# Sums of squares ahead of a norm: eight rows added on VectorE and one summed over the partitions on TensorE, in place of three

## The reference

```python
def _rmsnorm(x, g):
    x32 = x.astype(jnp.float32)
    y = x32 * lax.rsqrt(jnp.mean(jnp.square(x32), axis=-1, keepdims=True) + EPS)
    return (y * g.astype(jnp.float32)).astype(x.dtype)

def _modulate(x, g, shift, scale):
    return _rmsnorm(x, g) * (1.0 + scale) + shift

for l in range(DEPTH):
    ...
    x = x + gt1 * o                                                        # o: the mixed output times w_out
    x = x + gt2 * _swiglu(_modulate(x, g_ffn[l], sh2, sc2), w_ffn_in[l], w_ffn_out[l])
    ...                                                                    # xc likewise, in layer 0 alone
return _rmsnorm(x, g_final)
```

## Time and profile before

| what | us |
|---|---|
| median of 3 runs | 2006.08 (2005.21 to 2007.08) |
| profiled execution, its own time | 2007.02 |
| its span in the trace | 2005.2 |
| TensorE matmul busy | 1977.7 (99%) |
| TensorE weight load busy | 1671.6 (83%) |
| VectorE busy | 1354.1 (68%) |
| ScalarE busy | 898.5 (45%) |
| GpSimd busy | 821.0 (41%) |

### The profile page before, as it was taken

One profiled execution on the slowest core, in us unless ns is written; L12 is line 12 of the kernel. 1 busy time (PEld: TensorE's weight loads), 2 busy tenths in 40 slices (PEclk: granted clock), 3 DMA queues, 4 the chain that ended last, 5 costly groups with the idle time before them and its releaser, 6 DMA issues.

```text
span 2005.2 us, 29242 instructions
## 1 busy us (share of the span) xinstructions
PE 1977.7 (99%) x11034; PEld 1671.6 (83%) x11034; DVE 1354.1 (68%) x2356; ACT 898.5 (45%) x1400; POOL 821.0 (41%) x355
## 2 busy tenths in 40 slices
PE   8999999999999999999999999999999999999998
PEld 5778788888888778777878887777899999999997
DVE  5894644567878867787885544689747878644555
ACT  4787544322122252235222212589855344555444
POOL 1002322344434444444344443500546886454443
PEclk9999999999999999999999999999999999999999
DMA  8222211222222334543544452322323555454554
GB/s 339 81 84 84 84 44 62 84 92 97 88 101 84 105 126 184 192 154 141 207 172 180 179 210 102 148 82 78 135 106 128 188 188 187 171 188 156 185 187 146
DMA packets 38699, 278.32 MB, mean 139 GB/s; under 512 B 4416, under 2 KB 4416, under 8 KB 5312
## 3 DMA queue, kind: packets, MB, share of 16 engines
q1 hardware_dynamic: 38592, 276.87, 37.6%
HBM read 275.80 MB, written 1.05 MB: 138 GB/s over the span
## 4 chain that ended last, share of the span: by engine, by line
PE 91%; DVE 3%; ACT 2%; POOL 1%; issue 1%; DMA 1%; SPq 0%; DVEq 0%; POOLq 0%; ACTq 0%
PE PS L513 90%; POOL WL L468 1%; PE PS L786 1%; DMA RAW<-in_stream 1%; ACT WH L878 1%; DVE PS L1325 0%; DMA CD<-in_lruw 0%; DVE CD L1325 0%; ACT PS L878 0%; DVE PS L1328 0%; DVE LT L1328 0%; PE PS L611 0%; ACT TMP L878 0%; ACT HH L878 0%; DVE HL L1328 0%
## 5 line engine op out<-in xcount | busy, mean ns | idle before, releaser
L468 POOL TENSOR_TENSOR WL<-RAW,WH 128x1024 fp32r<-128x1024 f32 x336 | 809.8, 2429 | 1159.6 <-ACT WH L878 1159.4
L513 PE MATMUL PS<-HH,WH 128*128 128x512 f32 (+1 forms) x2272 | 797.6, 351 | 6.7 <-DVE CD L1325 1.8
L513 PE MATMUL PS<-HH,WL 128*128 128x512 f32 (+1 forms) x2272 | 778.2, 343 | 0.0
L513 PE MATMUL PS<-HL,WH 128*128 128x512 f32 (+1 forms) x2272 | 776.0, 343 | 0.4 <-DVE HL L1328 0.3
L878 ACT ACTIVATE WH<-RAW 128x1024 fp32r<-128x1024 f32 x416 | 417.8, 1052 | 664.8 <-PE PS L513 629.7
L513 PEld LDWEIGHTS PS<-HH,WH 128*128 128x128 f32 x2272 | 429.5, 189 | 72.0 <-issue 10.2
L513 PEld LDWEIGHTS PS<-HL,WH 128*128 128x128 f32 x2272 | 428.4, 189 | 60.2 <-issue 6.1
L513 PEld LDWEIGHTS PS<-HH,WL 128*128 128x128 f32 x2272 | 429.1, 189 | 55.5
L513 PE MATMUL PS<-ZH,WH 128*128 128x512 f32 (+1 forms) x992 | 336.6, 339 | 3.7 <-POOL WL L468 3.3
L513 PE MATMUL PS<-ZH,WL 128*128 128x512 f32 (+1 forms) x992 | 335.6, 338 | 0.0
L513 PE MATMUL PS<-ZL,WH 128*128 128x512 f32 (+1 forms) x992 | 335.6, 338 | 0.0
(11 more groups left out here) (180 smaller groups left out, 1642.4 us busy)
## 6 DMA issues: line engine op xcount, KB each, us to landing
RAW<-in_stream SPq DMA_DIRECT2D x208, 1024.0 KB, 4.8
G<-in_modw SPq DMA_DIRECT2D x22, 1024.0 KB, 7.0
CD<-in_modw SPq DMA_DIRECT2D x22, 1024.0 KB, 7.0
CD<-in_lruw SPq DMA_DIRECT2D x2, 2048.0 KB, 9.1
X<-in_xT SPq DMA_DIRECT2D x2, 1024.0 KB, 7.2
S<-in_modw SPq DMA_DIRECT2D x2, 1024.0 KB, 13.0
RAW<-in_modw SPq DMA_DIRECT2D x1, 1024.0 KB, 15.9
TMP<-in_modw SPq DMA_DIRECT2D x1, 1024.0 KB, 17.8
```

What stands on the lines that cost most here:

```text
L468: nc.gpsimd.tensor_tensor(WL[:, a:b], RAW[:, a:b], WH[:, a:b].bitcast(F32), ALU.subtract)\
L513: return nc.tensor.matmul(out, lhs, rhs, start=start, stop=stop)
```

## The change

For the norms that products follow (`after < DEPTH`) VectorE goes on with rows 6 and 7 behind the last residual, and writes the total of all eight rows to row 0 of `S`; TensorE waits for that and sums this one row over the partitions. The final norm keeps its form.

```diff
@@ stage_and_sums, TensorE @@
-                pe.wait_ge(L[after][nm + "_s"].sem if after < DEPTH else fin_s, KC - 3)
-                token_sums(row(S, 0, w), w, True, False)
-                square_sums(after, nm, w, range(KC - 2, KC)).then_inc(L[after][nm + "_p"].sem if after < DEPTH else fin_p, 1)
+                pe.wait_ge(L[after][nm + "_s"].sem if after < DEPTH else fin_s, KC - 1 if after < DEPTH else KC - 3)
+                last = token_sums(row(S, 0, w), w, True, after < DEPTH)
+                if after == DEPTH:
+                    last = square_sums(after, nm, w, range(KC - 2, KC))
+                last.then_inc(L[after][nm + "_p"].sem if after < DEPTH else fin_p, 1)
@@ added_and_summed, VectorE @@
+                    end = KC - 1 if after < DEPTH else KC - 3
+
+                    def summed(k):
+                        dve.wait_ge(sq, k + 1)
+                        if k > 1:
+                            dve.wait_ge(part, k - 1)
+                        tt(row(S, 0, W) if k == end else bank(7, W), bank(7, W), row(S, k, W), ADD).then_inc(part, 1)
+
                     for n in range(KC // 2):
                         s, m = n % 2, b + n // 2
                         for k in range(max(1, 2 * n - 2), 2 * n):
-                            dve.wait_ge(sq, k + 1)
-                            if k > 1:
-                                dve.wait_ge(part, k - 1)
-                            tt(row(S, 0, W) if k == KC - 3 else bank(7, W), bank(7, W), row(S, k, W), ADD).then_inc(part, 1)
+                            summed(k)
...
+                    for k in range(KC - 2, end + 1):
+                        summed(k)
```

## The result

The changed kernel takes 2009.4 us in the median of 12 runs, beside 2005.68 for the kernel before on the same chip: 3.7 us more. The ratio is 1.0017, or 3.4 us, with a 95% interval from 1.0009 to 1.0025, which is 1.8 to 5.0 us. Forecast were 2008.8 us and 0.13%. In a second set of runs the ratio was 1.0022 (1.001 to 1.0034). (One run of the first set, at 2764.89 us, was disturbed; the ratio leaves it out, and the median without it is 2009.29.)

The account below looks back on a forecast made before the run. TensorE's single queue of products was taken as the bound, lengthened only by waits such as the norms. The profiled 2007.02 + 1.98 (additions) + 0.70 (clock) = 2009.7 us, less 0.94 to the median: 2008.8, own range 2007.4 to 2010.2.

Parts of the forecast that it names:

- What bounds the kernel: TensorE is busy 99% of the span; only what makes it wait, such as the three norms, moves the end.
- Removed, nothing gained: Sums of rows 0 and 6 end as row 7's square does or sooner: removal gains nothing, at best 0.04 us.
- A: Feed-forward norm of layer 0, 512 tokens, 905.65 to 912.74 us: one addition and hand-over on the path, +0.75 us.
- Added: VectorE's row 6 addition is hidden at each norm; row 7's, with a hand-over, is not: 1.98 us together.
- Moved work: VectorE's modulation work stays hidden behind the wait for ScalarE's root: 0.98 us of wait left at A, 0.44 at B.
- B: Mixing norm of layer 1, 512 tokens, 1285.80 to 1293.74 us, clock already falling there: additions cost +0.75 us.
- Does it reach the end: Behind the norms, long stretches of products without a stop have no slack to give back: all the delay counts.
- C: Feed-forward norm of layer 1, 256 tokens, up to 1805.03 us: one addition and hand-over on the path, +0.48 us.
- The clock: The longer, emptier lull ahead of the norms adds one more fall of the granted clock in the typical run: 0.70 us.
- the second rival: The clock falls at all three norms, early enough to slow sums too: 3.4 us at least, 5.7 at most; 17%.
- free additions: At A and B TensorE's own sums or something other than the norm hold it: 2006.1 us, no change; 10%.
- slow old sums: The clock is low already during rows 0 and 6's sums at A and B; removing them gives 2003.9 us; 5%.

Follow-up runs that it names:

- the lags: Changed kernel with 12 (A, B) or 18 (C) unread VectorE additions ahead of the last two, one place per run: ratios to before 1.0076, 1.0079, 1.0068.
- row 7 alone: Kernel before, with TensorE summing only row 7's squares ahead of the three norms, rows 0 to 6 left out: 2008.26 us, ratio to before 1.0009.
- the halves: Kernel before, with VectorE adding row 6 ahead of the last residual and row 7 squared and summed in two halves for 512 tokens: 2004.89 us, ratio 0.9987.

## Why the prediction was right, and the term that was too small

**What bounds the kernel**: right. The three lines of dependences set the time; 7.6 us less of TensorE's busy time bought nothing. (The 5 us forecast were the loads' own length; the loads' busy time fell by 6.9.)

**Removed, nothing gained**: right. The tie at A was a tie; with rows 0 and 6 out the root came no sooner.

**Added**: right to a few hundredths. 0.74, 0.74 and 0.46 us for 0.75, 0.75 and 0.48; sums 2.38 us behind the last product's end for 2.4. Reading the price off the same instruction on earlier rows, and counting that row 6's addition fits beside the square, were enough. The longer variant of 2.3 us did not come.

**Moved work**: right. The reciprocal still waits for ScalarE, 1.07 us at A for 0.98 forecast. At B it is 1.53 for 0.44, since the root there is late by the clock as well.

**Does it reach the end**: right, as far as the lags can show it. What the prediction did not see is how much the stretch between B and C scatters from one execution to the next, 3.5 us over eleven traces, by TensorE's pace above all and by a few waits for late weights. With an earlier start it made the single profiled time 2.0 us less than the 2009.7 summed for it. The "long stretches of products without a stop" held from A to B and for a long while behind C; between B and C the trace of before had short stops, near 1570, 1725 and 1795 us, and the argument should have looked there. No lag shows them giving anything back.

**The clock**: the term that was mis-sized. One more fall, 0.70 us, was put in; the clock's part is 1.80. There are two parts to it, and the second rival, at 17%, had more of them than the forecast. A falls as well: the norm starts 0.50 us later by that. And at B the fall comes with the start of the sums and lasts twice as long: the sums take 0.81 us more, and the slow warm-up products ahead of the spread hold it up by 0.6, while the spread itself was slow in before already. The prediction priced a fall by the spread alone, and took the warm-up products as free because they are free at the full clock. The second rival's "at every place" is refuted by C, which stayed at 1.00, in both traces.
By the Trainium skill ("TensorE: Matmul & The Clock Gate", section "HAM oscillation") idle gaps between bursts of matmuls send the clock back, but the gaps that it warns of are longer than any at A and B of these two kernels, so by it neither would fall. The traces don't agree: A and B of the changed kernel fell with a gap of 2.37 us. Nor does the gap alone decide. With row 7 alone TensorE was idle for 1.72 us at A and B, and only B fell; in before B fell with TensorE busy for 3.87 of 4 us, and in the halves A fell with no gap of TensorE's loads above 0.3 us. Why A and B, which do the same work, differ in before stays open.

The result lay in the forecast's own range, 2007.4 to 2010.2, but that doesn't tell the forecast from the second rival, whose growth begins at 3.4 us where 3.7 was measured and 2.7 forecast. With the clock's term at 1.80 in place of 0.70 the prediction's own sum gives 3.8. Only the traces, with the additions as forecast, A and B low and C not, put the result between the two. Neither of the first and third rivals (free additions, slow old sums) left a trace. The third was priced with a slip, too: by its own sum, 2 x (0.75 - lag) + 0.48, the lag must pass 0.99 us, not 0.75, before the change pays.

## What to carry to other kernels

Work that another engine takes over is priced by the path: a hidden sum is worth nothing when removed, and the one addition that must wait for the last square costs its full length with its hand-over. Where TensorE's queue runs through a chain of small steps, read the granted clock there; filling the longer lull with unused products gave 2.8 us back here, while those that stood ahead of a ready operand at the lower clock cost half a microsecond at B. To shorten such a chain, cut the last step in pieces that start with the pieces before it, rather than move it to another engine: in the halves that brought the root 0.6 us forward at A and B. And before a difference of a few us is read from one pair of traces, compare the stretches that the change doesn't touch.

## What the runs showed of the hardware that was not expected

A busy share near 1 did not hold the clock at B. In before TensorE is busy for 3.87 of the 4 us from 1286 to 1290, mostly with one-column sums, and the clock falls at 1290, as it does with the lull empty (row 7 alone); the same records at A left it at 1.00. Four unused products of 256 columns in the changed kernel's lull kept it at 1.00 at both, in the one trace taken.

One-column records at the lower clock took 1.86 us for 8 in place of 1.05, nearly twice, though they stream one column each; the same 8 weight loads took 1.78 us for 0.97. So these one-column products went at the pace of their weight loads, and that was slow with the clock.

Products of 256 columns do not always go at one pace. With the clock shown as 1.00 and TensorE without idle time, they started 0.117, 0.119 or 0.120 us apart for 40 us and more in layer 1, in one execution and not in the next, for no cause that these traces show. Over a thousand products that is 2 to 3 us, as much as the change itself.
